# A bidirectional recurrence in four pairs of heads: the output of one pair and the preparation of the next in one stage

## The reference, cut to what matters

```
def step(S, inp):
    r_t, w_t, k_t, v_t, kk_t, a_t = inp
    s_kk = jnp.einsum('bhij,bhj->bhi', S, kk_t)
    S = (S * w_t[:, :, None, :] - s_kk[..., None] * (a_t * kk_t)[:, :, None, :]
         + v_t[..., None] * k_t[:, :, None, :])
    return S, jnp.einsum('bhij,bhj->bhi', S, r_t)
...
mean = jnp.mean(wkv, axis=-1, keepdims=True)
var = jnp.mean(jnp.square(wkv - mean), axis=-1, keepdims=True)
normed = ((wkv - mean) * lax.rsqrt(var + LNX_EPS)).reshape(B, T, RWKV_DIM)
normed = normed * ln_w.astype(f32) + ln_b.astype(f32)
```

## Time and profile before

| | before |
|---|---|
| median of 3 executions | 3814.72 us (3810.71 to 3820.34) |
| profiled execution, its own time | 3825.96 us |
| its span | 3824.1 us |
| TensorE busy | 3169.6 us (83%) |
| VectorE busy | 2125.8 us (56%) |
| ScalarE busy | 1340.5 us (35%) |
| GpSimd busy | 381.6 us (10%) |
| mean granted clock of TensorE | 0.893 |

### The profile page before, as it was taken

How to read it: one execution, slowest core, us unless ns; L and a number is a source line. 1 busy time by engine, 2 the same in 40 slices (tenths; PEclk the granted TensorE clock), 3 DMA queues, 4 the chain that set the end, 5 groups by cost and what they waited for, 6 DMA issues and landing times. The chain is left out here.

```text
span 3824.1 us, 58374 instructions
## 1 busy us (share of the span) xinstructions
PE 3169.6 (83%) x24565; PEld 2477.3 (65%) x24565; DVE 2125.8 (56%) x2592; ACT 1340.5 (35%) x1776; POOL 381.6 (10%) x249
## 2 busy tenths in 40 slices
PE   6699956679999899587987878858799872999995
PEld 1378845568888678473666574747566662888884
DVE  6632254356666533427366665767211347988885
ACT  1320143322111232327333333434200222777774
POOL 0200011210000000302011111111000000122120
PEclk7699967879999999799998888969899976999997
DMA  8131102211111323200201010010310334999996
GB/s 323 57 101 40 38 1 95 82 44 50 49 44 51 108 88 102 79 18 28 68 2 66 1 43 24 4 47 18 102 50 22 127 139 154 377 395 396 399 394 214
DMA packets 219997, 424.22 MB, mean 111 GB/s; under 512 B 13120, under 2 KB 122642, under 8 KB 219538
## 3 DMA queue, kind: packets, MB, share of 16 engines
q1 hardware_dynamic: 212434, 394.75, 29.0%
q0 software_dynamic: 4608, 16.78, 1.7%
q10 hardware_dynamic: 2753, 9.66, 0.6%
HBM read 387.61 MB, written 33.55 MB: 110 GB/s over the span
## 5 line engine op out<-in xcount | busy, mean ns | idle before, releaser
L213 DVE TENSOR_TENSOR w_exp_low<-w_exp,w_exp_high 128x2048 fp32r<-128x2048 f32 x192 | 437.7, 2290 | 54.2 <-ACT w_exp_high L208 54.2
L208 ACT ACTIVATE w_exp_high<-w_exp 128x2048 fp32r<-128x2048 f32 x192 | 368.0, 1920 | 123.2 <-PE psum L221 123.2
L219 PE MATMUL psum<-ffn_high,w_high 128*128 128x512 f32 x704 | 275.0, 391 | 9.2 <-DVE w_low L213 9.2
L220 PE MATMUL psum<-ffn_low,w_high 128*128 128x512 f32 x704 | 274.8, 390 | 0.0
L221 PE MATMUL psum<-ffn_high,w_low 128*128 128x512 f32 x704 | 274.8, 390 | 0.0
L1375 DVE SCALAR_TENSOR_TENSOR ffn_hidden<-u_padded,param_columns,ffn_hidden 128x1024 f32 (+1 forms) x176 | 226.2, 1285 | 23.8 <-DVE ffn_hidden L1371 0.2
L219 PE MATMUL psum<-w_exp_high,x_turned_high 128*128 128x512 f32 x512 | 202.9, 396 | 7.0 <-DVE w_exp_low L213 7.0
L221 PE MATMUL psum<-w_exp_high,x_turned_low 128*128 128x512 f32 x512 | 200.0, 391 | 0.0
L220 PE MATMUL psum<-w_exp_low,x_turned_high 128*128 128x512 f32 x512 | 199.8, 390 | 0.0
L2301 DVE COPY inverse<-psum 64x512 f32<-64x512 f32 x192 | 121.8, 637 | 75.5 <-PE psum L2136 50.4
L219 PE MATMUL psum<-ffn_down_w_split,ffn_down_lhs_split 128*128 128x512 f32 x352 | 140.6, 400 | 23.3 <-DVE ffn_down_lhs_split L213 17.4
(11 more groups left out here) (431 smaller groups left out, 7867.4 us busy)
## 6 DMA issues: line engine op xcount, KB each, us to landing
w_exp<-in_exp_w_gate SPq DMA_DIRECT2D x32, 2048.0 KB, 11.1
w_exp<-in_exp_w_up SPq DMA_DIRECT2D x32, 2048.0 KB, 10.4
w_exp<-in_exp_w_down SPq DMA_DIRECT2D x32, 2048.0 KB, 11.2
ada_weights<-in_w_ada SPq DMA_DIRECT2D x12, 2048.0 KB, 14.0
w_raw<-in_w_up SPq DMA_DIRECT2D x44, 512.0 KB, 3.8
ffn_down_ring<-in_w_down SPq DMA_DIRECT2D x44, 512.0 KB, 3.6
mix_out_ring<-in_w_out SPq DMA_DIRECT2D x32, 512.0 KB, 3.7
mixers_hT<-hidden SPq DMA_DIRECT2D x4, 4096.0 KB, 13.0
```

Source lines behind the costliest of these rows:

```text
L208: return nc.scalar.activation(out, src, ACT.Copy, scale=scale)
L213: return nc.vector.tensor_tensor(out, src, high.bitcast(F32), ALU.subtract)
L219: nc.tensor.matmul(out, left[0], right[0], start=start, stop=False)
L220: nc.tensor.matmul(out, left[0], right[1], start=False, stop=False)
```

## The change

A new stage, `stage_rwkv_between`, does the output of a pair and the preparation of the next. It stands at the three borders between pairs; the preparation of the first pair and the output of the last keep stages of their own. Its engines' lists are those of the two old stages, interleaved. On TensorE, the transposes and the gate come behind the projections of k and r and ahead of the bonus sums and the projection of v. On VectorE the output's sums come first, its scaling comes ahead of the decay loops, and its last two products behind the shifts of k and r. The root is taken as Exp(-0.5 Ln(x)), where the old stage had Sqrt and a reciprocal. New buffers keep the output's rows (28 to 36 KB of each partition) and the preparation's apart.

The reload of `hT` moves from the output stage to the chunk stage, on SyncE, behind the last step that uses the overlapping memory. The hardware loop over the first three pairs becomes a Python loop, so that all four are written out.

```
-def stage_rwkv_chunks(core):
+def stage_rwkv_chunks(core, hT):
...
+        hT_in = s.sem("hT_in")
+
+        @s.b.sync
+        def _(sp):
+            sp.wait_ge(z_mm, 2 * (TT - 2))
+            for j in range(2):
+                sp.wait_ge(inv_mm[j], TT // 2 * EVENTS)
+            sp.dma_start(hT[:], hT_in_dram(core)).then_inc(hT_in, 16)
+            sp.wait_ge(hT_in, 16)
...
-def stage_rwkv_out(core, hT, pr):
+def stage_rwkv_between(core, hT, pair, more):
...
+    NORM, W_UP, A_UP, TURNED, GATE, DOTS, NEXT = 0, (1, 2), (3, 0), 0, 1, 0, (1, 2, 3)
+    with Stage(core, "between") as s:
...
+            sp.dma_start(gup[:], dram["g_up_2"][0][:, pair * P:pair * P + P]).then_inc(gup_in, 16)
...
+            def output():
+                pe.wait_ge(scaled, 1)
+                pe.wait_ge(a_done, 2)
+                for t in range(TT):
+                    ins = nc.tensor.transpose(ps[:, 2 * TURNED + t // 4, (t % 4) * P:(t % 4 + 1) * P], yf[:, t],
+                                              core.mask(M_ID))
+                ins.then_inc(turned, 1)
+                pe.wait_ge(gup_in, 16)
+                if more:
+                    pe.wait_ge(shift, 1)
+                for h in range(2):
+                    ins = nc.tensor.matmul(ps[:, 2 * GATE + h, :], gup[:], core.lows[:, 0, 512 * h:512 * h + 512],
+                                           start=True, stop=True)
+                ins.then_inc(g_mm, 1)
+
+            pe.wait_ge(sq_done, 1)
+            over_heads(NORM).then_inc(norm_mm, 1)
+            pe.wait_ge(up_in, 64)
+            for d in range(2):
+                ups(0, d, W_UP[d]).then_inc(w_mm, 1)
+            ups(1, 0, A_UP[0]).then_inc(a_mm, 1)
+            pe.wait_ge(norm_cut, 1)
+            ups(1, 1, A_UP[1]).then_inc(a_mm, 1)
+            pe.wait_ge(sg_done, 1)
+            if more:
+                project(0)
+                pe.wait_ge(sg_done, 2)
+                project(1)
+            output()
+            pe.wait_ge(dots_in, 1)
+            pe.wait_ge(cm_out, 1)
+            over_heads(DOTS).then_inc(dots_mm, 1)
+            if more:
+                project(2)
+
+        @s.b.scalar
+        def _(act):
+            nc.scalar.preload_act_table(ACT.Sigmoid)
+            nc.scalar.activation(t1[:], k[:], ACT.Square, scale=col("k_k_2")).then_inc(sq_done, 1)
+            nc.scalar.activation(vc[:], core.next_v, ACT.Copy).then_inc(v_kept, 1)
+            act.wait_ge(centred, 1)
+            nc.scalar.activation(sq[:], yf[:], ACT.Square).then_inc(squared, 1)
+            for d in range(2):
+                act.wait_ge(w_mm, d + 1)
+                nc.scalar.activation(sg[d][:], bank2(W_UP[d]), ACT.Sigmoid, bias=col(("w0_f_2", "w0_b_2")[d])
+                                     ).then_inc(sg_done, 1)
+            for d in range(2):
+                act.wait_ge(a_mm, d + 1)
+                nc.scalar.activation(a[d][:], bank2(A_UP[d]), ACT.Sigmoid, bias=col(("a0_f_2", "a0_b_2")[d])
+                                     ).then_inc(a_done, 1)
+            act.wait_ge(norm_cut, 1)
+            nc.scalar.activation(kk[:], kk[:], ACT.Ln).then_inc(log_done, 1)
+            act.wait_ge(order, 4)
+            nc.scalar.activation(stat[:, 2], stat[:, 1], ACT.Ln).then_inc(logged, 1)
+            act.wait_ge(log_done, 1)
+            nc.scalar.activation(kk[:], kk[:], ACT.Exp, scale=-0.5).then_inc(root_done, 1)
+            act.wait_ge(logged, 1)
+            nc.scalar.activation(stat[:, 2], stat[:, 2], ACT.Exp, scale=-0.5).then_inc(rooted, 1)
+            for d in range(2):
+                act.wait_ge(scan_done, d + 1)
+                nc.scalar.activation(src[:, d, 1], b[d][:], ACT.Exp, scale=-DECAY_SCALE).then_inc(p_exp, 1)
+                nc.scalar.activation(e[d][:], b[d][:], ACT.Exp, scale=DECAY_SCALE).then_inc(m_exp, 1)
+
+            def follow_on(n):
+                act.wait_ge(rkv_mm, n + 1)
+                if n == 0:
+                    act.wait_ge(kk_done, 1)
+                    act.wait_ge(kd_done, 2)
+                if n == 1:
+                    act.wait_ge(dots_in, 1)
+                    act.wait_ge(p_used, 2)
+                if n == 2:
+                    act.wait_ge(v_kept, 1)
+                parts[n][0]()
+
+            if more:
+                follow_on(0)
+                follow_on(1)
+            act.wait_ge(turned, 1)
+            nc.scalar.activation(cm[:], bank2(TURNED), ACT.Identity, bias=col_of("ln_x_b_2", pair),
+                                 scale=col_of("ln_x_w_2", pair)).then_inc(cm_out, 1)
+            if more:
+                follow_on(2)
...
+        @s.b.vector
+        def _(dve):
+            nc.vector.tensor_tensor(yf[:], yf[:], yb[:], ALU.add).then_inc(summed, 1)
+            dve.wait_ge(summed, 1)
+            nc.vector.reduce_sum(stat[:, 0], by_head(yf), axis=AX).then_inc(order, 1)
+            dve.wait_ge(order, 1)
+            nc.vector.tensor_scalar(stat[:, 0], stat[:, 0], 1.0 / RN, None, ALU.mult).then_inc(order, 1)
+            dve.wait_ge(order, 2)
+            nc.vector.tensor_tensor(by_head(yf), by_head(yf), stat[:, 0].unsqueeze(2).to_broadcast([P, G, RN]),
+                                    ALU.subtract).then_inc(centred, 1)
+            dve.wait_ge(norm_mm, 1)
+            nc.vector.tensor_scalar(kk[:], bank2(NORM), 1e-24, None, ALU.max).then_inc(norm_cut, 1)
+            dve.wait_ge(squared, 1)
+            nc.vector.reduce_sum(stat[:, 1], by_head(sq), axis=AX).then_inc(order, 1)
+            dve.wait_ge(order, 3)
+            nc.vector.tensor_scalar(stat[:, 1], stat[:, 1], 1.0 / RN, LNX_EPS, ALU.mult, ALU.add).then_inc(order, 1)
+            for d in range(2):
+                dve.wait_ge(sg_done, d + 1)
+                way = slice(None) if d == 0 else slice(None, None, -1)
+                if d == 0:
+                    dve.wait_ge(reset_done, 3)
+                nc.vector.tensor_tensor_scan(b[d][:, way], reset[:, d, way], sg[d][:, way], 0.0,
+                                             ALU.mult, ALU.add).then_inc(scan_done, 1)
+            for d in range(2):
+                dve.wait_ge(a_done, d + 1)
+                nc.vector.tensor_scalar(src[:, d, 2], a[d][:], col("k_a_2"), core.one_ka[:, pr:pr + 1],
+                                        ALU.mult, ALU.add).then_inc(kd_half, 1)
+                dve.wait_ge(kd_half, d + 1)
+                nc.vector.tensor_tensor(src[:, d, 2], src[:, d, 2], k[:], ALU.mult).then_inc(kd_done, 1)
+            dve.wait_ge(rooted, 1)
+            nc.vector.tensor_tensor(by_head(yf), by_head(yf), stat[:, 2].unsqueeze(2).to_broadcast([P, G, RN]),
+                                    ALU.mult).then_inc(scaled, 1)
+            dve.wait_ge(kd_done, 2)
+            dve.wait_ge(norm_mm, 1)
+            nc.vector.tensor_tensor(t1[:], src[:, 0, 2], src[:, 1, 2], ALU.add).then_inc(sum_kd, 1)
+            dve.wait_ge(sum_kd, 1)
+            nc.vector.scalar_tensor_tensor(out=t1[:], in0=t1[:], scalar=col("r_k_2"), in1=r[:], op0=ALU.mult,
+                                           op1=ALU.mult).then_inc(dots_in, 1)
+            dve.wait_ge(root_done, 1)
+            nc.vector.scalar_tensor_tensor(out=kk[:], in0=k[:], scalar=col("k_k_2"), in1=kk[:], op0=ALU.mult,
+                                           op1=ALU.mult).then_inc(kk_done, 1)
+            dve.wait_ge(kk_done, 1)
+            for d in range(2):
...
+            if more:
+                parts[0][1]()
+                parts[1][1]()
+            dve.wait_ge(cm_out, 1)
+            nc.vector.tensor_tensor(cm[:], cm[:], bonus[:], ALU.add).then_inc(with_bonus, 1)
+            dve.wait_ge(with_bonus, 1)
+            dve.wait_ge(g_mm, 1)
+            nc.vector.tensor_tensor(core.yrT[:, pair, :], cm[:], bank2(GATE), ALU.mult).then_inc(out_done, 1)
+            dve.wait_ge(v_kept, 1)
+            dve.wait_ge(dots_mm, 1)
+            nc.vector.tensor_tensor(bonus[:], bank2(DOTS), vc[:], ALU.mult).then_inc(bonus_done, 1)
+            if more:
+                parts[2][1]()
...
+def stage_rwkv_out(core, pr):
...
-        hT_in = s.sem("hT_in")
 
         @s.b.sync
         def _(sp):
             sp.dma_start(gup[:], dram["g_up_2"][0][:, bass.ds(pr * P, P)]).then_inc(gup_in, 16)
-            sp.dma_start(hT[:], hT_in_dram(core)).then_inc(hT_in, 16)
-            sp.wait_ge(hT_in, 16)
...
 def rwkv_pairs(core, hT):
-    with core.nc.Fori(0, RH // 2 - 1) as pr:
-        stage_rwkv_prepare(core, hT, pr, True)
-        stage_rwkv_chunks(core)
-        stage_rwkv_out(core, hT, pr)
-    stage_rwkv_prepare(core, hT, RH // 2 - 1, False)
-    stage_rwkv_chunks(core)
-    stage_rwkv_out(core, hT, RH // 2 - 1)
+    pairs = RH // 2
+    stage_rwkv_prepare(core, hT, 0, True)
+    for pair in range(pairs):
+        stage_rwkv_chunks(core, hT)
+        if pair + 1 < pairs:
+            stage_rwkv_between(core, hT, pair, pair + 2 < pairs)
+    stage_rwkv_out(core, pairs - 1)
```

88 lines of the change are left out of this document (added).

## The result

| | before | after |
|---|---|---|
| median of 4 executions | 3814.69 us (3810.71 to 3820.34) | 3779.81 us (3771.59 to 3786.19) |
| profiled execution, its own time | 3825.96 us | 3777.56 us |
| its span | 3824.1 us | 3775.7 us |
| mean granted clock | 0.893 | 0.903 |

The ratio is 0.9906, 95% interval 0.9883 to 0.993: 34.9 us less. The forecast was 3778. Two repeats gave 3783.79 and 3781.03, at ratios of 0.9906 (0.9881 to 0.9931) and 0.9887 (0.9865 to 0.9909). One of the ten executions of experiment 2 took 5618 us, at a granted clock of 0.549; it is left out of that run's ratio.

What follows compares the result with a forecast made beforehand. No single engine: the output stage is a chain through three mostly idle engines, and TensorE sets the preparation's end. 44.80 - 5.8 - 3.85 + 1.5 = 36.6 us off the median 3814.72 gives 3778, range 3766 to 3793.

Steps and rivals of the forecast that it cites:

- Removed: At the borders between pairs: three output stages with their borders go, 44.80 us; the fourth stays.
- TensorE, 2.9 a stage: New stages with projections: transposes and gate matmuls ahead of the sums add 2.9 us each, 5.8 for both.
- VectorE's margin, 0.8: New stages with projections: VectorE's shift of k ends 0.8 us before TensorE comes to the gate matmuls that wait for it.
- Rival A: VectorE takes TensorE's place in the new stage, delaying gate, sums and projection of v: 6 us, 3784; chance 0.12.
- The third border, 3.85: Last new stage, without projections: scaling, bonus addition and gate product stay on VectorE's path, adding 3.85 us.
- The reload, nothing: Reload of hT in the chunks' tail: lands over 5 us before the stage ends, so it costs zero.
- Rival B: The reload disturbs the chunks' tail, making instruction fetches late: about 11 us over four tails, 3789; chance 0.12.
- C: A fetch stands behind the whole reload in each of four tails: 15 us slower, 3830; chance 0.02.
- Unrolling, 1.5: Preparations' entry: without the loop's back edge TensorE starts 0.74 us earlier, taken off twice, 1.5 us.
- The bound of 3: Upper bound of the gain from writing out the loop, with as much again on other queues; lower bound 0.
- Rival D: Output's chain returns serially at new stage's end: 35 us, about 3813 (experiment 8's text: 12 a stage); chance 0.04.
- What would show it wrong: Whole kernel: fewer than 25 us gone, or more than 5 us of the gain outside the borders between pairs.

Runs made afterwards that it cites:

- experiment 2: The kernel before, still in its loop, with only the reload of hT moved to the chunks' tail: 3821.98 us beside 3821.70, ratio 0.9995.
- experiment 1: The kernel before with its four pairs written out and nothing else changed: 3818.89 us beside 3821.70, ratio 0.9991.
- experiment 7: The fused kernel with four more VectorE passes behind the output's scaling, ahead of the decay loops, in each new stage: 3799.33 us, ratio 0.9943.
- experiment 8: The fused kernel with the output's transposes, gate, products and bonus sums behind the projection of v and its shift: 3781.51 us, ratio 0.9907.
- experiment 3: The fused kernel without the reload; GpSimd fills hT with zeros in its place: 3797.55 us, ratio 0.9936.
- experiment 6: The fused kernel with the reload at the head of the new stage, ahead of the projections' weights: 3803.17 us beside 3821.27, ratio 0.9953.
- experiment 4: The fused kernel with the reload done twice, the second behind the landing of the first: 3819.27 us, ratio 0.9993.

## Why the prediction was right, step by step

**Removed.** The three output stages, 44.80 us, went. Their work now stands in time that was idle, VectorE's sums in the head of the stage, or runs at the full clock, as the transposes and the gate do.

**TensorE, 2.9 a stage.** From the projections' start to the end, the written-out preparation takes 47.29 us (experiment 1, both) and the fused stage 49.92 (after and both repeats, six times): +2.63. Transposes and gate took 2.59 to the start of the sums (2105.78 to 2108.37), for 2.8 counted; the wait for the ScalarE copy, put at 0.1, vanished in it. Pipelined matmuls overlap at a seam; single durations added up count them too high (1.04 and 1.88 make 2.92, and start to start they take 2.59).

The first new stage took 59.74, and 60.73 and 59.68 in the repeats, for 61.6 forecast. The forecast had the projections begin 11.1 us behind the entry; they began at 9.82, 10.81 and 9.76. Most of what it came out too long by is thus where the clock rose in the head, for which the prediction had a spread of 1 to 2 us a stage and no term.

**VectorE's margin, 0.8.** It was 1.27 in after and 1.3 by experiment 7. Counted from the projections' start, k's first part began at 24.6 us for 25.1 counted (the output's scaling, 1.23 in the sum, put off the next start by 1.14), its second part stood 1.31 behind the first and not 1.42, and TensorE came to the gate at 28.4 for 28.65. Rival A's mechanism exists, names the row that it was said to name, and costs time once VectorE is late by more than 1.3 us. It did not come in. It also costs more than one for one, 1.7 us of lower clock on top, which the prediction lacked.

**The third border, 3.85.** 38.33 against 34.81 is +3.5; against experiment 1's 35.70 the mean of after and the repeats (38.51) is +2.8. The early work fitted by 0.50 us, for 0.3 predicted.

**The reload, nothing.** Issued at 2048.45 it landed 14.2 us later, 5.8 before the next entry (4 to 6 predicted). Rival B is against the rows: twice the load left the tail's pace as it was. So is C. That the load takes about 1 us longer where it now stands was in no term and fell under the cover.

**Unrolling, 1.5: the term that was mis-sized.** Only the first matmul of a preparation was read. Experiment 1 has 4.0 us less in the three borders than before, and 4.9 less than experiment 2, which keeps the loop. What repeats from row to row adds to 3.7: the first matmul 0.74 and 0.71 earlier, 0.32 less from the projections' start to the end, twice, and the output stages 14.39 where the loop has 15.01, 15.01 and 14.78. The rest, such as the 13.89 of the first one, goes with the clock. The bound of 3 was passed as well. Its total, -3.4 with an interval of about 4.7 either way, agrees and proves nothing. With the output stages at 42.67 in written-out form, and the new stages 3.07, 2.89 and 2.81 longer than its preparations (means of after and the repeats), fusing brings 33.9, give or take the us or so that the clock moves such a sum, and 4.0 + 33.9 = 37.9. (The first two, 2.98 on average, are over the 2.63 above by what the clock did ahead of the projections.) The prediction's 36.6 came out of 35.15 and 1.5: right in sum, a little shifted between its two terms.

**The closeness of 3778 to 3779.81** is partly luck. The interval leaves 27 to 45 us for the gain, and the three runs of this kernel gave 34.9, 37.5 and 42.7; the profiled borders alone gave 39.3, for 36.6 summed up.

**Rival D.** Its place was tried in experiment 8 and its price was wrong. The order within the fused stage is worth 0.8 us, to the other side, not 12. A price of 12 would need the whole chain, sums and scaling too, behind the projection of v; that was not tried.

**What would show it wrong.** More than 5 us of the gain outside the borders was named as a sign, and the two profiled executions have 9. The 3.7 of the chunk stages do not come back in the repeats. Outside the pairs it is less clear: the three kernels with separate stages take 3024.0 to 3027.1 us there (before, experiments 1 and 2), the nine fused ones 3018.4 to 3023.7, with the same code and the same number of instructions. But the part ahead of the first pair alone varies between 1877.1 and 1885.6 us among the fused ones. Whether some 4 us there belong to the change or to chance, these runs do not show; no term of the prediction has them. The medians lie 34.9, 37.5 and 42.7 us apart. The sign was set too tight for two single executions whose other code varies by that much. Sums from rows were right to a few us, and the clock's rise alone moved each new stage by up to 1.4.

## What to carry to other kernels

A stage whose engines wait for each other in a chain costs its latency; put into a stage that one other engine fills, it costs only what it adds to that engine, here 2.6 us for 15. Ask of a moved transfer what else then stands in its queue: at the head of the fused stage the same reload cost 9 us, in the tail nothing, and before the fusion its place did not matter at all. A stand-in for work left out needs a price of its own, or the run measures the stand-in.

## What the runs showed of the hardware that was not expected

A GpSimd memset of 32 KB a partition (6.92 us) stopped VectorE's TENSOR_SCALAR instructions begun within it until 0.1 us after its end, in all four tails: a row of two took 4.39 us instead of 0.41, and one more 3.76 instead of 0.28 (experiment 3). The Trainium skill (SBUF — State Buffer, "Who interferes with whom") says of a VectorE instruction in a mode that uses both port pairs that whichever of the two engines issues first gets the shared pair for the whole instruction, and that the other fully blocks. No row shows the mode. The 4.39 us agree with it for the first two, which read and write SBUF; the third reads PSUM and stands behind them, so its 3.76 may be only the wait for its turn. No run separates them. The five instructions that began within the memset ahead of these, products and sums with an input from PSUM, kept their length.

A wait of 3.6 us in the midst of a stage brought the granted clock from 1.00 to 0.68 over the next 5.3 us, and cost 1.7 us beyond itself (experiment 7). After the 7.54 us of waiting in experiment 6 it was 0.61 over the next 3.7 us.

The 4 MB reload took 13.0 us beside the output stage and 13.9 to 14.5 in every run that issues it in the chunks' tail, also where most of it ran after the last output (experiment 4), while the tail itself did not slow. TensorE's first matmul stood 2.49 to 2.50 us behind the entry in every written-out preparation, in every fused stage and in the loop's first pass, and 3.21 to 3.66 in its second and third (before and experiment 2).
